# Forgetting attention of a streaming encoder: scores as two products with stacked query parts and the decay sums in rows of their own

## The chip, the cores and the metric

The kernel runs on one core of a Trainium2 chip. The metric is the device time of one execution in microseconds. A core has five engines with instruction queues of their own: PE (TensorE, matrix products; its weight loads are shown as PEld), DVE (VectorE), ACT (ScalarE), POOL (GpSimd) and SP (SyncE, which here only issues DMAs). Each engine works its queue in order. They wait for each other through semaphores.

## The reference

One step of a two-layer encoder: 512 new frames of a prompt stream and 32 frames of a running stream with 512 cached frames (544 frames in all, width 1024). The first layer has latent attention, the second forgetting attention, each between feed-forward blocks. What matters here is the second attention: 16 heads of width 64, and a logit bias that is the difference of two running sums of log forget gates.

```python
c_k = jnp.cumsum(logf_all, axis=1).transpose(0, 2, 1)
c_q = c_k[:, :, -l:]
q = _rms_norm((hn @ p['w_b_q'][j]).reshape(b, l, B_HEADS, B_HD), p['g_b_qn'][j])
o = _attention(q, k_all, v_all, pos, k_pos, False, c_q, c_k)
# in _attend:
s = jnp.einsum('bqhd,bkhd->bhqk', q, k, preferred_element_type=jnp.float32) * (q.shape[-1] ** -0.5)
s = s + (c_q[:, :, :, None] - c_k[:, :, None, :])
s = jnp.where(mask[None, None], s, -jnp.inf)
p = jax.nn.softmax(s, axis=-1).astype(v.dtype)
return jnp.einsum('bhqk,bkhd->bqhd', p, v)
```

The mask is causal by frame. The running stream's 32 frames attend to the 512 cached ones and to each other.

## The kernel before, in words

All arithmetic is in float32 accuracy on an engine path that rounds its operands. So every operand x is held as a high part (x rounded, made by ACT) and a low part (x minus the high part, made by DVE), and a product takes three matmuls: high by high, high by low, low by high. This is `product`, L600 to L604.

The kernel works in stages, each written as one program per engine: feed-forward F0, latent projection, first attention, output projection, F1, shared keys and values (KV), F2, query projection (Q), second attention, output projection, F3, final norm. Nothing reorders the instructions: what stands in a queue is the order in which the functions are called, and semaphore counts with names (`Steps`) tie the queues together.

The second attention is a loop over 8 pairs of heads (`pair_b` on PE, ACT, DVE and POOL; L1003, L1549, L2216, L2595, and the SP loop at L577). A turn p finishes pair p's second head (head 1), makes pair p + 1 ready ("staging") and does the scores of its first head (head 0):

- SP loads pair p + 1's keys and values from DRAM into SBUF, token by token (L571 to L574), each time after the buffer before it is free.
- PE turns keys and queries to have the head's width on the partitions (`staged`, L874; `staged_samples`, L882 for the 32 frames of the running stream); ACT and DVE split the result into high and low parts, `qT` and `kT` (`stage_part`, L1468 and L2126). In the profile `kT` is named x_hi and x_lo, whose memory it shares.
- Scores come in five groups u (`scores`, L885): u = 0 to 3 are four blocks of 128 queries against 128 x (u + 1) keys, u = 4 is the 32 running frames in two halves of 272 keys. Each group is a `product` and the mask, added by a matmul with the identity (L905, L912). DVE takes the row maximum (L2022), ACT the exponential (L1401), POOL divides by the row sum (L2571), PE turns the probabilities (L926), ACT and DVE split them, and PE multiplies them by the values (`values`, L946).
- The bias is inside the product: queries and keys have 66 rows, 64 of the head and two more. A query carries (1, sum at the query), a key (minus the sum at the key, 1). POOL copies the sums `cs` and `ncs` beside the heads (L2537, L2540), they are turned with them, and the gain column of the queries has ones in rows 64 and 65 (DVE memset at L1912).

Score groups use banks 0 to 2 of PSUM, and a group waits for the exponential of the group that had its bank before. The turns of keys, queries and probabilities share banks 3 to 5 (`w_uses`), and each waits for the splits of what the bank held.

The query projection ahead of it has eight units m of weights (L1147): PE multiplies five token tiles by the unit's weights, ACT rounds the next unit's weights (L1170), DVE makes their low part (L1722) and takes the finished half of the queries (L2336).

Of the kernel before, what the change touches and what calls it, by code (L numbers as in the profile page):

```python
# [19 lines left out]
ALU = mybir.AluOpType  # L20
# [20 lines left out]
DBX = DB + 2  # L41
# [37 lines left out]
class Steps:  # L79
# [81 lines left out]
    "dve": ["wlo", "fs0", "fs1", "b", "min", "u", "w", "z", "a", "wz", "rb", "eb", "l", "lf", "c", "negc"]}  # L161
FSTAGE = {"pool": ["q", "cq", "ck"]}
# [4 lines left out]
def build(nc, d):  # L167
    with ExitStack() as ctx:
# [81 lines left out]
        qn = place("q_normed", [P, NT, HEADS, DB])  # L250
        at_[0] = start + 4 * 7840
        cs = place("forget_sum", [P, NK, HEADS])
        ncs = place("forget_sum_neg", [P, NK, HEADS])
# [68 lines left out]
        def tile(t, k):  # L322
# [8 lines left out]
        k_loaded, v_loaded, stored = sem("k_loaded"), sem("v_loaded"), sem("stored")  # L331
        stored_lf = sem("stored_log_forget")
        stored_kv = [sem("stored_kv0"), sem("stored_kv1")]
        set_dve, set_act, set_pool = sem("setup_dve"), sem("setup_act"), sem("setup_pool")
# [4 lines left out]
                     forget=FORGET, fstage=FSTAGE, resplit=RESPLIT, relow=RELOW, yout=YOUT)  # L339
# [26 lines left out]
        def ffn(f, gain):  # L366
            parts = []
            for hf in range(HALVES):
# [4 lines left out]
                if hf == 1:  # L373
# [28 lines left out]
                 att=run("attx", PAIRS), out=run("out", PAIRS), fstage=run("fstage", PAIRS))  # L402
# [57 lines left out]
        def _(sp):  # L460
# [101 lines left out]
            ksx = ks[:, 0:NK * 2 * DBX].rearrange("p (t g w) -> p t g w", t=NK, g=2)  # L562
# [33 lines left out]
        def _(pe):  # L596
# [177 lines left out]
            pe.wait_ge(set_dve, 5)  # L774
# [39 lines left out]
            def attention(L, mla, mask):  # L814
                att, stg, stq, D = L["att"], L["stage"], L["stageq"], L["d"]
                prq, prk = L.get("projq"), L.get("projk")
                qsv = qs[:, 0:NT * 2 * D].rearrange("p (t g w) -> p t g w", t=NT, g=2)
                ksv = ks[:, 0:NK * 2 * D].rearrange("p (t g w) -> p t g w", t=NK, g=2)
# [42 lines left out]
                def staged(name, it, uses, before, first=False):  # L861

                    v, t0 = {"q": (qsv, 0), "p": (ksv, 0), "c": (ksv, NT)}[name[0]]
                    if not mla and name == "q0":
                        pe.wait_ge(*L["fstage"]["pool"].at("ck", it))
                        pe.wait_ge(k_loaded, 16 * 6 * (it + 1))
# [6 lines left out]
                    for t in range(4):  # L873
                        mm = pe.transpose(ps[0:D, b, t * P:(t + 1) * P], v[:, t0 + t, int(name[1]), :], ident[:, :])  # L874
                    mm.then_inc((stq if name[0] == "q" else stg)["pe"].sem, 1)

                def staged_samples(it, uses, before=None):
                    b = [x[1] for x in uses if x[0] == "ts"][0] if before is None else bank_of("ts", uses, before)
                    for n, v in enumerate((qsv, ksv)):
                        for g in range(2):  # L880
                            o = (2 * n + g) * DEC
                            mm = pe.transpose(ps[0:D, b, o:o + DEC], v[S0:P, 4, g, :], ident[S0:P, S0:P])  # L882
                    mm.then_inc(stg["pe"].sem, 1)

                def scores(hh, u, p, first=False):  # L885
# [14 lines left out]
                    q = [a[0:D, hh * T + TS[u]:hh * T + TS[u] + P] for a in qT]  # L900
                    k = [a[0:D, hh * KEYS:(hh + 1) * KEYS] for a in kT]
                    if u < 4:
                        out = ps[:, u % 3, 0:P_W[u]]
                        product(out, q, [a[:, 0:P_W[u]] for a in k], True, False)
                        mm = pe.matmul(out[:, u * P:(u + 1) * P], identr[:, :], mask[:, :], start=False, stop=True)  # L905
                    else:
                        for n in range(2):
                            c = SEQ + n * HALF_T
                            mm = product(ps[:, 1 + n, 0:HALF_T], q, [a[:, c:c + HALF_T] for a in k], True,
                                         mla or n == 0)  # L910
# [235 lines left out]

            for m in range(8):  # L1147
# [15 lines left out]
        def _(act):  # L1163
# [169 lines left out]
            act.wait_ge(set_dve, 7)  # L1333
# [53 lines left out]
            def attention(L, mla, g_q, g_k):  # L1387
# [74 lines left out]
                def stage_part(name, it, first=False):  # L1462
# [5 lines left out]
                    act.activation(out[0][0:D, hh * n + o:hh * n + o + SEQ], ps[0:D, b, :], ACT.Copy, **kw  # L1468
                                   ).then_inc(st["act"].sem, 1)

                def stage_samples(it, first=False):
                    inc, b = stg["act"].sem, (FIRST_BANKS if first else banks)["ts"]
                    act.wait_ge(*stg["pe"].at("ts", it))
                    for n, (out, g) in enumerate(((qT, g_q), (kT, g_k))):
                        w = T if n == 0 else KEYS
                        kw = {} if g is None else {"scale": g[0:D, :]}
                        act.activation(out[0][0:D, :].rearrange("p (g w) -> p g w", g=2)[:, :, w - DEC:w],
                                       ps[0:D, b, n * 2 * DEC:(n + 1) * 2 * DEC
                                          ].rearrange("p (g w) -> p g w", g=2), ACT.Copy, **kw).then_inc(inc, 1)

# [68 lines left out]
                def pair_b(p, first, stages):  # L1549
# [68 lines left out]
                else:  # L1618
                    for name in ("q0", "p0", "p1", "c0", "q1", "c1"):
                        stage_part(name, 0)  # L1620
                    stage_samples(0)
                    for u in range(5):
# [78 lines left out]
            for m in range(8):  # L1701
# [3 lines left out]
                if m == 5:  # L1705
                    square_queries(0)
            square_queries(1)
# [7 lines left out]
        def _(dve):  # L1715
# [196 lines left out]
            dve.memset(gbq[DB:DB + 2, :], 1.0).then_inc(set_dve, 1)  # L1912
# [97 lines left out]
            def attention(L, mla, g_q, g_k, meanwhile=None):  # L2010
# [109 lines left out]
                def stage_part(name, it, first=False):  # L2120
# [3 lines left out]
                    dve.wait_ge(*st["act"].at(name, it))  # L2124
                    c = slice(hh * n + o, hh * n + o + SEQ)
                    low(out[1][0:D, c], ps[0:D, b, :], out[0][0:D, c], None if g is None else g[0:D, :], st["dve"].sem)  # L2126

                def stage_samples(it, first=False):
                    b = (FIRST_BANKS if first else banks)["ts"]
                    for n, (out, g, w) in enumerate(((qT, g_q, T), (kT, g_k, KEYS))):  # L2130

                        dve.wait_ge(*stg["act"].at("sk", it))
                        o = [x[0:D, :].rearrange("p (g w) -> p g w", g=2)[:, :, w - DEC:w] for x in out]
                        low(o[1], ps[0:D, b, n * 2 * DEC:(n + 1) * 2 * DEC
                                     ].rearrange("p (g w) -> p g w", g=2), o[0],
                            None if g is None else g[0:D, :], stg["dve"].sem)
# [247 lines left out]
            for m in range(16):  # L2384
# [56 lines left out]
                if m == 10:  # L2441
# [4 lines left out]
                    dve.tensor_scalar(ncs[:, :, :], o, -1.0, None, ALU.mult).then_inc(finc, 1)  # L2446
# [21 lines left out]
            for m in range(8):  # L2468
# [11 lines left out]
                if m == 6:  # L2480
                    normalise(Q["k"][0], qv[0])
            take_chunk(Q["k"][1], U + 7, 1, qv[1].rearrange("p t g w -> p t (g w)"))
# [12 lines left out]
        def _(pool):  # L2495
# [30 lines left out]
            def attention(L, mla, meanwhile=None):  # L2526
                att, stg, D = L["att"], L["stage"], L["d"]
                prq, prk = L.get("projq"), L.get("projk")
                qsv = qs[:, 0:NT * 2 * D].rearrange("p (t g w) -> p t g w", t=NT, g=2)
                ksv = ks[:, 0:NK * 2 * D].rearrange("p (t g w) -> p t g w", t=NK, g=2)  # L2530

                def stage_fox(it):
# [6 lines left out]
                    for dst, src, n in ((qsv[:, :, :, DB + 1], cs, NT), (ksv[:, :, :, DB], ncs, NK)):  # L2539
                        pool.tensor_copy(dst, src[:, 0:n, bass.ds(it * 2, 2)]).then_inc(inc, 1)  # L2540
# [124 lines left out]
            qx = qs[:, 0:NT * 2 * DBX].rearrange("p (t w) -> p t w", w=DBX)  # L2665
            kx = ks[:, 0:NK * 2 * DBX].rearrange("p (t w) -> p t w", w=DBX)
            pool.memset(qx[:, :, DB:DB + 1], 1.0).then_inc(set_pool, 1)
            pool.memset(kx[:, :, DB + 1:DB + 2], 1.0).then_inc(set_pool, 1)
# [111 lines left out]
```

## Time and profile before

| | us |
|---|---|
| median of 3 runs | 2368.77 (2368.72 to 2372.03) |
| profiled execution, its own time | 2368.68 |
| span of the profile, first to last instruction | 2366.5 |
| busy: PE / DVE / ACT / POOL | 2233.0 / 1719.0 / 1076.0 / 322.4 |
| mean granted clock of PE | 0.972 of full speed |

The profile is of one execution. A timeline row gives the start of an instruction and how long it took; matmuls overlap in the array, so the time that one costs is the distance from its start to the next one's, not its duration. An idle time in brackets is that of the engine just before the instruction, with what ended it. "Granted clock" is the share of full speed at which PE was clocked; it has two levels here, 1.0 and 0.5 (2.4 and 1.2 GHz), and its column lags behind the matmuls by some us.

### The profile page before, as it was taken

How to read it: one execution, taken by the hardware profiler on the slowest of the kernel's cores; microseconds unless marked ns; L12 is line 12 of the kernel's file. 1: busy time of each engine (PE TensorE's matmuls, PEld its weight loads, DVE VectorE, ACT ScalarE, POOL GpSimd, SP SyncE). 2: the span in 40 equal slices, each digit the busy share in tenths (PEclk: the TensorE clock that was granted, in tenths of full speed). 3: DMA queues.
4: the chain of work that ended last, by engine and by line, in shares of the span. 5: the costliest groups of instructions: out<-in, count | busy, mean ns of one | idle time of the engine just before them, and what ended most of it. 6: DMA issues, size and time to landing. Idle time of an engine off the chain costs nothing. (4 is left out here: it accounts for less than half of the span.)

```text
span 2366.5 us, 45430 instructions
## 1 busy us (share of the span) xinstructions
PE 2233.0 (94%) x16514; PEld 2147.5 (91%) x16514; DVE 1719.0 (73%) x2708; ACT 1076.0 (45%) x1801; POOL 322.4 (14%) x281
## 2 busy tenths in 40 slices
PE   4999999889988899999999999999989998999997
PEld 4999999889988899999977999999868888999997
DVE  7985984578875896697455984995358858966973
ACT  5542543456764553354224551453247745533531
POOL 1000002035551100000122000001043321000001
PEclk9999999989988999999999999999979989999998
DMA  2222232100002232222223322222222212222221
GB/s 99 101 96 91 103 104 84 47 20 20 14 19 72 72 106 86 87 104 98 76 75 108 108 108 97 89 95 83 72 54 53 58 45 86 91 102 85 106 91 62
DMA packets 72801, 187.44 MB, mean 79 GB/s; under 512 B 40720, under 2 KB 42288, under 8 KB 61440
## 3 DMA queue, kind: packets, MB, share of 16 engines
q1 hardware_dynamic: 71424, 181.67, 22.7%
q0 software_dynamic: 1280, 4.49, 0.5%
q8 instruction: 59, 0.97, 0.2%
q14 instruction: 38, 0.31, 0.0%
HBM read 178.79 MB, written 7.35 MB: 79 GB/s over the span
## 5 line engine op out<-in xcount | busy, mean ns | idle before, releaser
L602 PE MATMUL ps<-xs_hi,w_hi 128*128 128x272 f32 x1408 | 410.3, 291 | 50.2 <-DVE w_lo_more L1752 31.9
L604 PE MATMUL ps<-xs_hi,w_lo 128*128 128x272 f32 x1408 | 408.0, 290 | 0.0
L603 PE MATMUL ps<-xs_lo,w_hi 128*128 128x272 f32 x1408 | 407.2, 289 | 0.0
L1170 ACT ACTIVATE w_hi<-raw 128x1408 fp32r<-128x1408 f32 (+4 forms) x123 | 146.0, 1188 | 506.1 <-PE ps L627 246.2
L1199 ACT ACTIVATE w_hi<-w_blocks 128x1024 fp32r<-128x1024 f32 x176 | 186.8, 1062 | 323.5 <-PE ps L604 157.8
L602 PEld LDWEIGHTS ps<-xs_hi,w_hi 128*128 128x128 f32 x1408 | 266.5, 189 | 54.1 <-issue 29.9
L602 PE MATMUL ps<-xs_hi,w_hi_more 128*128 128x272 f32 x1056 | 306.5, 290 | 2.4 <-ACT scratch L1245 1.8
L603 PE MATMUL ps<-xs_lo,w_hi_more 128*128 128x272 f32 x1056 | 305.9, 290 | 0.0
L627 PE MATMUL ps<-hid_hi,w_hi 128*128 128x272 f32 x1312 | 273.0, 289 | 9.1 <-DVE w_lo L1722 5.4
L627 PE MATMUL ps<-hid_lo,w_hi 128*128 128x272 f32 x1312 | 271.9, 289 | 0.0
L627 PE MATMUL ps<-hid_hi,w_lo 128*128 128x272 f32 x1312 | 271.8, 289 | 0.0
L604 PEld LDWEIGHTS ps<-xs_hi,w_lo 128*128 128x128 f32 x1408 | 267.1, 190 | 0.0
L603 PEld LDWEIGHTS ps<-xs_lo,w_hi 128*128 128x128 f32 x1408 | 266.7, 189 | 0.0
L1752 DVE TENSOR_TENSOR w_lo<-w_blocks,w_hi 128x1024 fp32r<-128x1024 f32 x176 | 215.2, 1223 | 28.3 <-ACT w_hi L1199 26.7
L1874 DVE SCALAR_TENSOR_TENSOR scratch<-ps,rstd 128x544 f32<-128x544 f32 x64 | 46.3, 724 | 257.0 <-PE ps L627 223.9
L627 PEld LDWEIGHTS ps<-hid_hi,w_hi 128*128 128x128 f32 x1312 | 207.4, 189 | 11.1 <-issue 11.1
L1722 DVE TENSOR_TENSOR w_lo<-raw,w_hi 128x1408 fp32r<-128x1408 f32 (+4 forms) x123 | 170.3, 1386 | 58.0 <-ACT w_hi L1170 57.8
L627 PEld LDWEIGHTS ps<-hid_hi,w_lo 128*128 128x128 f32 x1312 | 207.4, 189 | 0.0
L627 PEld LDWEIGHTS ps<-hid_lo,w_hi 128*128 128x128 f32 x1312 | 207.3, 189 | 0.0
L602 PEld LDWEIGHTS ps<-xs_hi,w_hi_more 128*128 128x128 f32 x1056 | 200.6, 190 | 3.9 <-ACT scratch L1245 2.7
L604 PE MATMUL ps<-xs_hi,w_lo_more 128*128 128x272 f32 x704 | 204.0, 290 | 0.0
L603 PEld LDWEIGHTS ps<-xs_lo,w_hi_more 128*128 128x128 f32 x1056 | 200.3, 190 | 0.1
(261 smaller groups left out, 5069.1 us busy)
## 6 DMA issues: line engine op xcount, KB each, us to landing
w_blocks<-w_ffn_in SPq DMA_DIRECT2D x88, 1024.0 KB, 4.8
raw<-w_ffn_out SPq DMA_DIRECT2D x64, 704.0 KB, 4.1
raw<-w_b_kv SPq DMA_DIRECT2D x16, 512.0 KB, 3.6
raw<-w_a_out SPq DMA_DIRECT2D x8, 512.0 KB, 3.6
raw<-w_b_q SPq DMA_DIRECT2D x8, 512.0 KB, 3.5
raw<-w_b_out SPq DMA_DIRECT2D x8, 512.0 KB, 3.6
raw<-w_a_in SPq DMA_DIRECT2D x4, 672.0 KB, 4.0
raw<-w_a_qup SPq DMA_DIRECT2D x8, 288.0 KB, 2.8
```

Source lines behind the costliest of these rows:

```text
L602: pe.matmul(out, lhs[0], rhs[0], start=start, stop=False, skip_group_check=more)
L603: pe.matmul(out, lhs[0], rhs[1], start=False, stop=False, skip_group_check=more)
L604: return pe.matmul(out, lhs[1], rhs[0], start=False, stop=stop, skip_group_check=more)
L627: mm = pe.matmul(pair(bank)[:, n, :], w[a], xs[b][:, cols], start=(k == 0 and a + b == 0), stop=(k == kt - 1 and a == 1))
L1170: act.activation(wh[par][:, 0:n], raw[par][:, 0:n], ACT.Copy).then_inc(w_hi, 1)
L1199: act.activation(wgroup[name][0], sources(par, name), ACT.Copy).then_inc(q["ws"]["act"].sem, 1)
L1722: dve.tensor_tensor(wl[par][:, 0:n], raw[par][:, 0:n], wh[par][:, 0:n].bitcast(F32), ALU.subtract).then_inc(w_lo, 1)
L1752: dve.tensor_tensor(lo, sources(par, name), hi.bitcast(F32), ALU.subtract).then_inc(q["ws"]["dve"].sem, 1)
L1874: dve.scalar_tensor_tensor(two(scratch[2]), pair(2 + j), -0.5, two(rstd[:, :]), ALU.mult, ALU.mult).then_inc(inc, 1)
```

## The change

Only the second attention and what prepares it is touched.

- Queries: rows 0 to 63 of `qT[0]` hold the high part and rows 64 to 127 the low part. `qT[1]` holds the high part again in rows 0 to 63 and two rows of decay sums and two of -1 behind them. ACT rounds the queries into `qT[1]`, DVE writes the low part into the lower half of `qT[0]`, and ACT copies the high part over (`queries_twice`, two copies of 64 x 544 a pair).
- Keys: SP loads each key twice, side by side, so that the turned keys have 128 rows; `kT[0]` has the high part in both halves. `kT[1]` has the low part in rows 0 to 63, two rows of ones and two of decay sums.
- Scores: `qT[0]` by `kT[0]` (128 rows) and `qT[1]` by `kT[1]` (68 rows): two matmuls for what took three. The product's decay terms are (sum at the query, high and low) x 1 and -1 x (sum at the key, high and low).
- Decay sums: in the query projection PE turns `cs` (`turn_decay`, three steps after units 3, 4 and 5), ACT and DVE split it, SP stores both parts in DRAM, and in each turn of its loop SP loads the pair's rows into `kT[1]` and `qT[1]` with six DMAs, after PE's last score group of the pair before. PE waits for them ahead of the first score of head 0.
- POOL no longer copies sums beside the heads; `ncs` is gone. It fills the rows of ones.

```diff
-DBX = DB + 2
+DBX = 2 * DB
+DBK = DB + 4
...
+        q_heads = place("q_heads", [P, NT, 2, DB + 2])[:, :, :, :]
+        k_heads = arena[:, 0:NK * 4 * DB].rearrange("p (t g w) -> p t g w", t=NK, g=2)
+        at_[0] = start + 4 * 6400
+        decay = [at_col("decay_hi", C_ARENA + nq + nk + nv, KEYS, F32R)[0:HEADS, :],
+                 place("decay_lo", [HEADS, KEYS], F32R)[:, :]]
         at_[0] = start + 4 * 7840
         cs = place("forget_sum", [P, NK, HEADS])
-        ncs = place("forget_sum_neg", [P, NK, HEADS])
...
-                    sp.dma_start(dst[:, 0:4, g, 0:DB], d[new_p].rearrange("(t p) e -> p t e", p=P)[:, :, cols]
-                                 ).then_inc(loaded_, 16)
-                    sp.dma_start(dst[S0:P, 4, g, 0:DB], d[new_s][:, cols]).then_inc(loaded_, 16)
-                    sp.dma_start(dst[:, NT:NK, g, 0:DB], d[old].rearrange("(t p) e -> p t e", p=P)[:, :, cols]
-                                 ).then_inc(loaded_, 16)
+                    for to, src in ((dst[:, 0:4, g], d[new_p].rearrange("(t p) e -> p t e", p=P)[:, :, cols]),
+                                    (dst[S0:P, 4, g], d[new_s][:, cols]),
+                                    (dst[:, NT:NK, g], d[old].rearrange("(t p) e -> p t e", p=P)[:, :, cols])):
+                        for n in range(to.shape[-1] // DB):
+                            sp.dma_start(to[..., n * DB:(n + 1) * DB], src).then_inc(loaded_, 16)
+
+            sp.wait_ge(*X["decay"]["dve"].at("sample"))
+            for n in range(2):
+                sp.dma_start(d["decay"][n], decay[n][:, :].bitcast(F32)).then_inc(decay_stored, 16)
...
+                sp.wait_ge(decay_stored, 32)
+                sp.wait_ge(decay_ones, 3)
+                sp.wait_ge(*X["att"]["pe"].at("s14", p - 1))
+                for n in range(2):
+                    heads = d["decay"][n:n + 1, bass.ds(2 * p, 2), :]
+                    rows = kT[1][DB + 2 + n:DB + 3 + n, :].bitcast(F32).rearrange("p (g w) -> p g w", g=2)
+                    sp.dma_start(rows, heads).then_inc(decay_loaded, 16)
+                    rows = qT[1][DB + n:DB + n + 1, :].bitcast(F32).rearrange("p (g w) -> p g w", g=2)
+                    for o, c, w in ((0, 0, SEQ), (SEQ, SEQ + PAST, DEC)):
+                        sp.dma_start(rows[:, :, o:o + w], heads[:, :, c:c + w]).then_inc(decay_loaded, 16)
...
-                    q = [a[0:D, hh * T + TS[u]:hh * T + TS[u] + P] for a in qT]
-                    k = [a[0:D, hh * KEYS:(hh + 1) * KEYS] for a in kT]
+                    if not mla and hh == 0 and u == 0:
+
+                        pe.wait_ge(decay_loaded, 16 * 6 * (p + 1))
+                    if not mla and u == 0:
+                        pe.wait_ge(*L["twice"]["act"].at(f"q{hh}", p))
+                    rows = (D, D) if mla else (P, DBK)
+                    q = [a[0:r, hh * T + TS[u]:hh * T + TS[u] + P] for a, r in zip(qT, rows)]
+                    k = [a[0:r, hh * KEYS:(hh + 1) * KEYS] for a, r in zip(kT, rows)]
+
+                    def times(out, k, stop):
+                        if mla:
+                            return product(out, q, k, True, stop)
+                        pe.matmul(out, q[0], k[0], start=True, stop=False)
+                        return pe.matmul(out, q[1], k[1], start=False, stop=stop)
+
                     if u < 4:
                         out = ps[:, u % 3, 0:P_W[u]]
-                        product(out, q, [a[:, 0:P_W[u]] for a in k], True, False)
+                        times(out, [a[:, 0:P_W[u]] for a in k], False)
...
+            def turn_decay(n):
+
+                st = X["decay"]
+                if n == 0:
+                    pe.wait_ge(*Q["rtok"]["dve"].at("rtok"))
+                else:
+                    pe.wait_ge(*st["dve"].at(DECAY["dve"][n - 1]))
+                if n < 2:
+                    for t in range(4):
+                        mm = pe.transpose(ps[0:HEADS, MISC, t * P:(t + 1) * P], cs[:, t if n == 0 else NT + t, :],
+                                          ident[:, :])
+                else:
+                    mm = pe.transpose(ps[0:HEADS, MISC, 0:DEC], cs[S0:P, 4, :], ident[S0:P, S0:P])
+                mm.then_inc(st["pe"].sem, 1)
...
+                if m in (3, 4, 5):
+                    turn_decay(m - 3)
...
+                def queries_twice(hh, it):
+
+                    act.wait_ge(*stq["act"].at(f"q{hh}", it))
+                    act.wait_ge(*stg["act"].at("sq", it))
+                    c = slice(hh * T, (hh + 1) * T)
+                    act.activation(qT[0][0:DB, c], qT[1][0:DB, c], ACT.Copy).then_inc(L["twice"]["act"].sem, 1)
...
                         stage_samples(p + 1)
+                        queries_twice(0, p + 1)
                     split_p(1, 0, p)
+                    if stages:
+                        queries_twice(1, p + 1)
...
+                    n, name = m - 3, DECAY["act"][m - 3]
+                    act.wait_ge(*X["decay"]["pe"].at(name))
+                    o, w = (n * SEQ, SEQ) if n < 2 else (SEQ + PAST, DEC)
+                    act.activation(decay[0][:, o:o + w], ps[0:HEADS, MISC, 0:w], ACT.Copy
+                                   ).then_inc(X["decay"]["act"].sem, 1)
...
+                    elif name[0] == "q":
+                        dve.wait_ge(*st["act"].at(name, it))
+                        low(out[0][DB:P, c], ps[0:DB, b, :], out[1][0:DB, c], g[0:DB, :], st["dve"].sem)
+                    else:
+                        dve.wait_ge(*st["act"].at(name, it))
+                        low(out[1][0:DB, c], ps[0:DB, b, :], out[0][0:DB, c], None, st["dve"].sem)
...
+                    n, name = m - 3, DECAY["dve"][m - 3]
+                    dve.wait_ge(*X["decay"]["act"].at(name))
+                    o, w = (n * SEQ, SEQ) if n < 2 else (SEQ + PAST, DEC)
+                    low(decay[1][:, o:o + w], ps[0:HEADS, MISC, 0:w], decay[0][:, o:o + w], None, X["decay"]["dve"].sem)
...
-                    for dst, src, n in ((qsv[:, :, :, DB + 1], cs, NT), (ksv[:, :, :, DB], ncs, NK)):
-                        pool.tensor_copy(dst, src[:, 0:n, bass.ds(it * 2, 2)]).then_inc(inc, 1)
...
+                    pool.wait_ge(*L["fstage"]["pool"].at("q", 0))
+                    pool.memset(kT[1][DB:DBK, :].bitcast(F32), 1.0).then_inc(decay_ones, 1)
+                    pool.wait_ge(decay_ones, 3)
```

The order of the instructions was read in three places. First SP, its loop over the pairs, before:

```order
L571 DMA arena<-o_k_p 128x4x64
L573 DMA arena<-o_k_s 32x64
L574 DMA arena<-fox_k 128x4x64
L582 REGISTER_ALU
L571 DMA arena<-o_v_p 128x4x64 [waits stagev_pool]
L573 DMA arena<-o_v_s 32x64
L574 DMA arena<-fox_v 128x4x64
L571 DMA arena<-o_v_p 128x4x64
L573 DMA arena<-o_v_s 32x64
L574 DMA arena<-fox_v 128x4x64
L577 REGISTER_ALU
L577 COMPARE_AND_BRANCH
```

and after; `decay` is the DRAM copy of the sums, `x_lo` is `kT[1]`:

```order
L585 DMA arena<-fox_v 128x4x64
L601 ISA [waits decay_ones,decay_stored]
L605 ISA [waits attx_pe]
L605 DMA x_lo<-decay 1x2112
L608 DMA qT_lo<-decay 1x2x512
L608 ISA
L608 DMA qT_lo<-decay 1x2x32
L605 ISA
L605 DMA x_lo<-decay 1x2112
L608 DMA qT_lo<-decay 1x2x512
L608 ISA
L608 DMA qT_lo<-decay 1x2x32
```

Six loads of decay rows now stand behind the six loads of values (only the last of these is shown here) in each turn, with waits for `decay_ones`, `decay_stored` and PE's last score group of the pair before; the key loads, ahead of the values, are twelve.

Second PE, the first score group of the next pair in a turn, before:

```order
L926 MATMUL ps<-ident,arena 128x128 [waits stage_dve]
L926 MATMUL ps<-ident,arena 128x128 x2
L899 REGISTER_ALU [waits attx_act]
L602 MATMUL ps<-x_hi,qT_hi 128x128 [waits stage_dve]
L603 MATMUL ps<-x_lo,qT_hi 128x128
L604 MATMUL ps<-x_hi,qT_lo 128x128
L905 MATMUL ps<-mask_causal,identr 128x128
L926 MATMUL ps<-ident,arena 128x128 [waits stage_dve]
```

and after:

```order
L968 MATMUL ps<-ident,arena 128x128 [waits stage_dve]
L968 MATMUL ps<-ident,arena 128x128 x2
L929 REGISTER_ALU [waits attx_act]
L932 REGISTER_ALU [waits stage_dve]
L934 REGISTER_ALU [waits decay_loaded]
L942 MATMUL ps<-x_hi,qT_hi 128x128 [waits twice_act]
L943 MATMUL ps<-x_lo,qT_lo 128x128
L948 MATMUL ps<-mask_causal,identr 128x128
L968 MATMUL ps<-ident,arena 128x128 [waits stage_dve]
```

The third matmul of a group is gone, and a wait for `decay_loaded` stands ahead of the first. The rest of PE's queue is behind it, the next score groups and the value products of head 1 among them.

Third ACT, in the query projection, with rounding of weights (`w_hi`) and squares of the queries, before:

```order
L1170 ACTIVATE w_hi<-raw_49 128x1024 [waits w_used,w_load0]
L1170 ACTIVATE w_hi<-raw_50 128x1024 [waits w_used,w_load1]
L1170 ACTIVATE w_hi<-raw_49 128x1024 [waits w_used,w_load0]
L1170 ACTIVATE w_hi<-raw_50 128x1024 [waits w_used,w_load1]
L1170 ACTIVATE w_hi<-raw_49 128x1024 [waits w_used,w_load0]
L1647 ACTIVATE scratch<-q_normed 128x2048 [waits tokq_dve]
L1649 ACTIVATE rstd<-q_normed 128x512
L1170 ACTIVATE w_hi<-raw_50 128x1024 [waits w_used,w_load1]
```

and after:

```order
L1229 ACTIVATE w_hi<-raw_50 128x1024 [waits w_used,w_load1]
L1229 ACTIVATE w_hi<-raw_49 128x1024 [waits w_used,w_load0]
L1788 ACTIVATE decay_hi<-ps 16x512 [waits decay_pe]
L1229 ACTIVATE w_hi<-raw_50 128x1024 [waits w_used,w_load1]
L1788 ACTIVATE decay_hi<-ps 16x512 [waits decay_pe]
L1229 ACTIVATE w_hi<-raw_49 128x1024 [waits w_used,w_load0]
L1724 ACTIVATE scratch<-q_normed 128x2048 [waits tokq_dve]
L1726 ACTIVATE rstd<-q_normed 128x512
```

ACT's first copy of decay sums stands ahead of the rounding of a unit's weights, the second ahead of the next.

## Rows read from the trace of the kernel before

**Rows 1.** Stages: one of six alike of the second attention's loop
```profile
core 0: us, PE busy (x) PEld busy (x) DVE busy (x) ACT busy (x) POOL busy (x), PEclk, DMA share, GB/s
...
1880.00:1900.00 20.00, 18.91 (x141) 16.54 (x141) 16.25 (x43) 15.01 (x42) 6.83 (x9) 1.00 0.22 54
```
**Rows 2.** Timeline of PE: start us, us, engine line op out<-in [idle before <-releaser]
```profile
1780.09 0.33 PE L602 MATMUL ps<-x_hi,qT_hi 66*128 66x128 f32 x1
...
1800.01 0.33 PE L602 MATMUL ps<-x_hi,qT_hi 66*128 66x128 f32 x1
...
1809.82 0.44 PE L602 MATMUL ps<-hid_hi,x_hi 128*128 128x384 f32 x1 [0.57 <-DVE x_lo L1732]
...
1812.24 0.30 PE L602 MATMUL ps<-x_hi,qT_hi 66*128 66x128 f32 x1
...
1812.49 0.28 PE L604 MATMUL ps<-x_hi,qT_lo 66*128 66x128 f32 x1
1812.60 0.28 PE L905 MATMUL ps<-mask_causal,identr 128*128 128x128 f32 x1
...
1815.23 0.39 PE L604 MATMUL ps<-x_hi,qT_lo 66*128 66x512 f32 x1
1815.46 0.23 PE L905 MATMUL ps<-mask_causal,identr 128*128 128x128 f32 x1
...
1816.89 0.28 PE L604 MATMUL ps<-x_hi,qT_lo 66*128 66x272 f32 x1
1817.01 0.18 PE L912 MATMUL ps<-mask_causal,identr 128*128 128x32 f32 x1
...
1899.50 0.33 PE L602 MATMUL ps<-x_hi,qT_hi 66*128 66x128 f32 x1
```
**Rows 3.** Timeline of DVE in the same turn
```profile
1802.74 0.56 DVE L2022 TENSOR_REDUCE stat<-ps 128x1 f32<-128x384 f32 x1 [0.26 <-PE ps L905]
...
1816.96 0.28 DVE L1732 TENSOR_TENSOR hid_lo<-ps,hid_hi 128x128 fp32r<-128x128 f32 x1
```
**Rows 4.** Timelines of ACT and of POOL in the same turn
```profile
1804.53 0.62 ACT L1460 ACTIVATE x_hi<-arena 128x512 fp32r<-128x512 f32 x1
...
1812.27 0.98 ACT L1410 ACTIVATE hid_hi<-ps 128x512 fp32r<-128x512 f32 x2 [0.95 <-PE ps L926]
...
1805.23 1.28 POOL L2577 TENSOR_TENSOR x_lo<-arena,x_hi 128x512 fp32r<-128x512 f32 x1 [5.74 <-ACT x_hi L1460]
```
**Rows 5.** Timeline of SP in the same turn, first and last of six value loads
```profile
1806.54 0.37 SPq L571 DMA_DIRECT2D arena<-o_v_p  x1
...
1809.12 0.38 SPq L574 DMA_DIRECT2D arena<-fox_v  x1
```
**Rows 6.** DMA issues from 1780 to 1900 us: count, KB each, median us to landing
```profile
arena<-fox_v SPq DMA_DIRECT2D x12, 128.0 KB, 2.5
...
arena<-o_v_s SPq DMA_DIRECT2D x12, 8.0 KB, 2.0
```
**Rows 7.** Timelines of PE and of ACT ahead of and in turn 0
```profile
1704.64 0.50 PE L602 MATMUL ps<-w_hi,x_hi 128*128 128x512 f32 x1 [0.35 <-DVE q_normed L2336]
...
1765.90 0.77 PE L602 MATMUL ps<-hid_hi,x_hi 128*128 128x512 f32 x1 [4.66 <-POOL x_lo L2577]
...
1701.60 1.06 ACT L1170 ACTIVATE w_hi<-raw 128x1024 fp32r<-128x1024 f32 x1 [7.01 <-PE ps L604]
```
**Rows 8.** Two holes of PE, and stages: mean granted clock is PEclk
```profile
1233.87 0.50 PE L602 MATMUL ps<-w_hi,x_hi 128*128 128x512 f32 x1 [3.10 <-DVE kv_chunk L2336]
...
1299.99 0.36 PE L602 MATMUL ps<-xs_hi,w_hi 128*128 128x272 f32 x1 [3.32 <-DVE w_lo_more L1752]
...
1234.00:1254.00 20.00, 20.00 (x102) 17.45 (x103) 10.22 (x9) 4.35 (x3) 6.79 (x1) 0.88 0.27 83
1300.00:1320.00 20.00, 19.59 (x140) 19.18 (x141) 18.60 (x25) 10.31 (x16) 1.31 (x2) 0.91 0.35 113
1744.00:1772.00 28.00, 22.08 (x94) 18.40 (x93) 15.84 (x35) 12.17 (x31) 19.81 (x16) 0.57 0.10 23
```

More of the change, by code:

```diff
@@ L338, in build @@
                      stage=STAGE, stageq=STAGEQ, projq=PROJQ, projk=PROJK, first=FIRST, latent=LATENT, tokn=TOKN, tokq=TOKQ, tokq1=TOKQ1, tokv=TOKV, rtok=RTOK,
-                     forget=FORGET, fstage=FSTAGE, resplit=RESPLIT, relow=RELOW, yout=YOUT)
+                     forget=FORGET, fstage=FSTAGE, twice=TWICE, decay=DECAY, resplit=RESPLIT, relow=RELOW, yout=YOUT)
         sems = {(k, e): sem(f"{k}_{e}") for k, v in kinds.items() for e in v}
@@ L401, in build @@
         X = dict(d=DBX, stage=run("stage", PAIRS), stageq=run("stageq", PAIRS), stagev=run("stagev", PAIRS), head0=run("head0x", PAIRS),
-                 att=run("attx", PAIRS), out=run("out", PAIRS), fstage=run("fstage", PAIRS))
+                 att=run("attx", PAIRS), out=run("out", PAIRS), fstage=run("fstage", PAIRS),
+                 decay=run("decay"), twice=run("twice", PAIRS))
         XO = dict(kind="out", what="supdate", u=units(KC, KC * P), kt=KC, st=run("supdate", DK),
@@ L771, in token_rstd @@
                 mm.then_inc(step.sem, 1)
-            pe.wait_ge(set_dve, 5)
+            pe.wait_ge(set_dve, 4)
             ffn_all(F0)
@@ L908, in scores @@
                             c = SEQ + n * HALF_T
-                            mm = product(ps[:, 1 + n, 0:HALF_T], q, [a[:, c:c + HALF_T] for a in k], True,
-                                         mla or n == 0)
+                            mm = times(ps[:, 1 + n, 0:HALF_T], [a[:, c:c + HALF_T] for a in k], mla or n == 0)
                         if not mla:
@@ L1467, in stage_part @@
                     kw = {} if g is None else {"scale": g[0:D, :]}
-                    act.activation(out[0][0:D, hh * n + o:hh * n + o + SEQ], ps[0:D, b, :], ACT.Copy, **kw
-                                   ).then_inc(st["act"].sem, 1)
+                    c = slice(hh * n + o, hh * n + o + SEQ)
+                    if mla or name[0] != "q":
+                        act.activation(out[0][0:D, c], ps[0:D, b, :], ACT.Copy, **kw).then_inc(st["act"].sem, 1)
+                    else:
+                        act.activation(out[1][0:DB, c], ps[0:DB, b, :], ACT.Copy, scale=g[0:DB, :]
+                                       ).then_inc(st["act"].sem, 1)
                 def stage_samples(it, first=False):
@@ L1621, in attention @@
                     stage_samples(0)
+                    queries_twice(0, 0)
+                    queries_twice(1, 0)
                     for u in range(5):
@@ L2132, in stage_samples @@
                         dve.wait_ge(*stg["act"].at("sk", it))
[L2133 to L2136, printed above, removed]
+                        o = [x.rearrange("p (g w) -> p g w", g=2)[:, :, w - DEC:w] for x in out]
+                        if mla:
+                            r, o = slice(0, D), [x[0:D] for x in o]
+                        else:
+                            r, o = slice(0, DB), [o[1][0:DB], o[0][DB:P]] if n == 0 else [x[0:DB] for x in o]
+                        low(o[1], ps[r, b, n * 2 * DEC:(n + 1) * 2 * DEC].rearrange("p (g w) -> p g w", g=2), o[0],
+                            None if g is None else g[r, :], stg["dve"].sem)
                 def split_units(it):
@@ L2664, in _ @@
             pool.wait_ge(*KV["k"][1]["dve"].at("ss"))
[L2665 to L2668, printed above, removed]
+            pool.wait_ge(*Q["rms"]["pe"].at("stat"))
+            pool.memset(qT[1][DB:DBK, :].bitcast(F32), -1.0).then_inc(decay_ones, 1)
+            pool.wait_ge(decay_ones, 1)
+            pool.memset(q_heads[:, :, :, DB:DB + 2], 0.0).then_inc(decay_ones, 1)
             pool.memset(vrv[0:S0, 4], 0.0).then_inc(vpad, 1)
@@ L2771 @@
     d |= {n: nc.dram_tensor(n, s, F32, kind="ExternalOutput").ap() for n, s in OUTS.items()}
+    d["decay"] = nc.dram_tensor("decay", (2, HEADS, KEYS), F32, kind="Internal").ap()
     build(nc, d)
```

56 lines of the change are left out of this document (36 added, 20 removed).

## The prediction

> **What bounds the kernel now.** I read the stages first: from 1780 to 1900 us six stretches of 20 us are all but alike, with PE busy 18.9 us of 20 at a granted clock of 1.00, DVE 16.2, ACT 15.0 [rows 1] (the last of the six). Then the timeline of PE inside one stretch. The loop of the second attention handles a pair of heads per turn. I call T0 the start of the first score of head 1 in a turn. T0 is 1780.09 in one turn, 1800.01 in the next and 1899.50 six turns after the first [rows 2], so a turn takes (1899.50 - 1780.09) / 6 = 19.90 us. PE has few holes: the last matmul before the value product of 384 columns waited 0.57 us for DVE's x_lo [rows 2]. So the turn is bounded by PE with DVE close behind.
>
> **The removed product.** In each score group the third product (L604) goes. Its price is the distance to the next start, since matmuls overlap: 0.11 us for 128 columns (1812.49 to 1812.60), 0.23 for 512 (1815.23 to 1815.46), 0.12 for 272 (1816.89 to 1817.01) [rows 2]. Widths 256 and 384 lie between: I take 0.11 and 0.18. A head has 128, 256, 384, 512 and twice 272: 0.11 + 0.11 + 0.18 + 0.23 + 0.24 = 0.87 us, 1.74 a turn. Eight turns would give 14 us if PE alone set the time. The two products that stay have 128 and 68 rows in place of 66. The distances above go by columns, so I price the taller operands at 0, between -0.1 and +0.1 a turn.
>
> **How much of that reaches the end of a turn.** I cut the turn at the first score of the next pair (head 0, group 0), which starts at 1812.24, that is T0 + 12.23 [rows 2]. Ahead of it 0.87 us of products go. But DVE sets this part: after its last short wait (0.26 us for PE at 1802.74, [rows 3]) it runs without a hole of note until the staged keys are split, and PE's wait at 1809.82 is for that. DVE can start at most that 0.26 earlier, plus about 0.1 for group 0: PE comes to T0 + 11.9. Behind the cut there are 19.90 - 12.23 = 7.67 us. 0.87 us of products go here too, but the last value products wait for DVE's low half of the turned probabilities, which ends at 1816.96 + 0.28 = 1817.24 [rows 3], just ahead of them. Its chain (four row maxima, three splits) begins with the first score and gets shorter only by what PE delays in it. Bounds: 6.8 (all 0.87) and 7.67 (nothing); I take 7.1, about two thirds of the saving.
>
> **The added loads on SP.** This is the term that decides. A turn of SP was: six loads of keys, a wait for POOL's split of the values, six loads of values. Now twelve, wait, six, and then six rows of decay sums, whose landing the first score of the next pair waits for. SP issues in order, so these six stand behind the six value loads. When do the value loads start? ACT copies the values at 1804.53 for 0.62 us, POOL splits them from 1805.23 for 1.28 us, and SP issues its first value load at 1806.54, T0 + 6.53 [rows 4, 5]. Nothing of the change makes that earlier: ACT works without a hole from the turn's start to there. The last value load is issued at 1809.12 + 0.38 = 1809.50; six loads thus take 2.96 us, 0.53 from one to the next [rows 5]. The decay rows: six DMAs, the last one issued 5 x 0.53 = 2.65 us after the first, the first 0.1 us after the values. Landing: an 8 KB load lands 2.0 us after its issue, a 128 KB load 2.5 us [rows 6]; a decay row (at most 8.4 KB) is nearest to the first. Another 0.2 us until PE starts. From the first value load: 2.96 + 0.1 + 2.65 + 2.0 + 0.2 = 7.9 us, so the first score starts at T0 + 6.53 + 7.9 = T0 + 14.4, while PE is there at T0 + 11.9. PE waits 2.5 us, and DVE and ACT, whose next row maximum and exponential hang on this score, with it. A turn becomes 14.4 + 7.1 = 21.5 us, 1.6 more than 19.9. No trace shows the issue of a DMA into one partition: bounds are 0.45 us each with 1.8 to land (T0 + 13.9) and 0.6 each with 3.0 to land (T0 + 15.8).
>
> **The other edits of a turn.** ACT gets two copies of queries, 64 x 544 from SBUF; the copy of 512 columns took 0.62 us [rows 4], so 0.65 each. The first falls into ACT's hole of 0.95 us at 1812.27 [rows 4], the second behind it, both while PE waits for the decay rows: 0 us; without that cover the first would still end at about T0 + 11.95, where PE comes, and cost at most 0.3. The doubled keys turn with the same transposes (moving operand is the identity, 128 columns) and the same ACT copy, 512 columns: 0. POOL loses two short copies that nobody waits for: 0. Twelve key loads on SP start behind the decay rows, at about T0 + 12.5, take 6.4 us and have landed by T0 + 21.5; staging asks for them in the following turn, behind four score groups: 0.
>
> **Ahead of the loop.** The decay sums are turned during the query projection: nine transposes on PE, at 0.1 us each 0.9 us. The first four sit after unit 3, and ACT's first decay copy (16 x 512, priced like a 512-column copy, 0.6 us) stands ahead of the split of unit 5's weights, which starts at 1701.60 and leads through DVE's split to the take of the projected queries; DVE has a low half of its own ahead of that. PE already waits there 0.35 us at 1704.64 [rows 7]. PE's transposes 0.5, ACT 0.6 and about 0.1 of handover push that chain by 1.2 us, and it is on the path. The other five transposes add 0.6: +1.8 us. POOL's memset of the ones rows (about 2.2 us) and the first decay loads end near 1740, before the first score of pair 0: 0. Then come five score groups at half clock (mean granted clock 0.57 from 1744 to 1772, [rows 8]), where a product costs double: (0.11 + 0.11 + 0.18) x 2 = 0.8 us up to group 2, on whose exponential group 4 waits for its bank, and 0.48 in group 4, together -1.3, of which ACT's two copies ahead of the first exponential take back 0.1: -1.2. So PE's long wait for POOL, ending at 1765.90 [rows 7], moves by +0.6. From there the value loads of pair 1 begin (0.2 us earlier than PE starts), 1766.3, plus 7.9 gives the first score at 1774.2, plus 7.1 gives T0 of turn 1 at 1781.3 against 1780.09: +1.2. Six turns: 6 x 1.6 = 9.9 us (unrounded 1.65). The last turn stages nothing and waits for values and DVE: 0. Sum +11.1 us. The profiled execution took 2368.68 us (span 2366.5 and 2.2 around it), the median of the runs is 2368.77: 2379.8, rounded 2380.
>
> **Rivals.**
> B, the clock: a hole of 2.5 us of PE in every turn lets the granted clock fall. For: after a hole of 3.32 us at 1299.99 the mean clock over the next 20 us was 0.91. Against: after 3.10 us at 1233.87 it was 0.88 in the next 20 us though the fall there came late, and holes of 0.6 us leave it at 1.00 [rows 8, 1]. So holes near 3 us stand at the edge. The clock's fall shows in the stretch behind the hole, which is the 7.1 us that PE mostly sets; 0.91 over 20 us is 3.6 us at half clock, and as much or twice that behind each hole would add 1.8 to 2.5 us a turn (not all of a turn's end is PE's), in six turns +13: 2393. The Trainium skill (TensorE: Matmul & The Clock Gate, HAM oscillation) says that a loop whose every tile waits for a DMA starts every tile at the lower of the two clocks; by that rule B would be the case in each turn, and the traces so far bear it out in part.
> C, the other side: the decay rows land before PE asks. It decides at T0 + 11.9, that is 5.4 us after the first value load; the value loads take 2.96 and the landing 2.0, which leaves 0.4 us for six issues, against 0.53 for one. If it held (or if SP ran its wait for the values much earlier than now), a turn would gain 0.3 + 0.6 = 0.9 us: +0.6 - 0.6 - 6 x 0.9 = -5.4, 2363.
> D, the PE saving is small and the wait hidden in part (issue and landing at their lower bounds, tail 6.8): a turn 20.7, +0.8: with the prologue about 2374.
>
> **Numbers.** A with its bounds 55 in 100 (own range 2374 to 2391), B 22, D 13, C 10. The range holds A, B and most of D: 2370 to 2397. A measurement of this kernel tells 0.2%, 4.7 us, from no change. C is mostly faster (0.08), the lower end of D and upper end of C same (0.08), the rest slower (0.84).
>
> **What would show it.** Right: in the timeline of PE a hole of 2 to 3.5 us ahead of the first score of head 0 in each turn, named as waiting for a DMA into x_lo or qT_lo; SP's value loads at T0 + 6.5 with six decay loads behind them; turns of 21 to 22.5 us; the score groups with two products at the distances above. The clock column decides between A and B: 1.00 or below 0.9 in the turns. Wrong: turns below 19.9 us, or decay loads that land before T0 + 12; a wait ahead of the first score that names ACT's copy of queries would show another cause; a shift of more than 3 us at the first transposes of pair 0 would show the decay turns mispriced.

## The result, and the profile after

| | us |
|---|---|
| before, median of the runs beside it | 2368.74 (2368.30 to 2372.03) |
| after, median of 4 runs | 2394.18 (2391.41 to 2405.25) |
| ratio after to before | 1.0116, 95% interval 1.0099 to 1.0133 |
| profiled execution of after, span, mean clock of PE | 2393.64, 2391.7, 0.964 |

The change makes the kernel 25.4 us slower. The forecast was slower by 11, to 2380. The direction and the place are as forecast, and the size is more than double. I read the profile after in the order of before: stages, then PE in one turn, then the queue that PE waits for. Three stretches of 23 us, each about a turn long, have the columns of [rows 1]:

```profile
core 0: us, PE busy (x) PEld busy (x) DVE busy (x) ACT busy (x) POOL busy (x), PEclk, DMA share, GB/s
1783.00:1806.00 23.00, 18.95 (x128) 16.25 (x126) 16.75 (x43) 15.80 (x43) 7.56 (x10) 0.93 0.32 72
...
1829.00:1852.00 23.00, 19.42 (x121) 16.61 (x120) 16.83 (x43) 15.81 (x43) 7.59 (x10) 0.85 0.32 72
...
1875.00:1898.00 23.00, 19.41 (x123) 16.43 (x122) 16.26 (x42) 15.10 (x43) 6.83 (x10) 0.87 0.30 67
```

A turn takes 23.1 to 25.7 us where it took 19.9, every engine has more idle time, and the granted clock, 1.00 before, is 0.93 in the first two of the six turns and falls to 0.78 in the last. The timeline of PE shows both causes a few rows apart. T0 of this turn is 1805.82:

```profile
1805.82 0.33 PE L942 MATMUL ps<-x_hi,qT_hi 128*128 128x128 f32 x1
...
1808.45 0.50 PE L942 MATMUL ps<-x_hi,qT_hi 128*128 128x512 f32 x1 [0.34 <-ACT arena L1460]
1808.78 0.39 PE L943 MATMUL ps<-x_lo,qT_lo 68*128 68x512 f32 x1
1809.01 0.22 PE L948 MATMUL ps<-mask_causal,identr 128*128 128x128 f32 x1
...
1815.25 0.44 PE L627 MATMUL ps<-hid_hi,x_hi 128*128 128x384 f32 x1 [0.54 <-DVE x_lo L1815]
...
1820.35 0.32 PE L942 MATMUL ps<-x_hi,qT_hi 128*128 128x128 f32 x1 [2.37 <-DMA qT_lo<-decay]
...
1821.33 0.63 PE L942 MATMUL ps<-x_hi,qT_hi 128*128 128x384 f32 x1
1821.75 0.52 PE L943 MATMUL ps<-x_lo,qT_lo 68*128 68x384 f32 x1
1822.07 0.31 PE L948 MATMUL ps<-mask_causal,identr 128*128 128x128 f32 x1
```

First, PE waits 2.37 us for a decay row ahead of head 0's first score (1820.35, T0 + 14.53). Over the six turns these waits sum to 14.0 us:

```profile
engine line waited for: us in total, times, longest us
...
PE ps L942 <- DMA qT_lo<-decay: 14.0, 6, 2.4
```

Second, behind the hole matmuls take longer. A product of 384 columns starts 0.42 us ahead of its successor (1821.33 to 1821.75) and a 68-row one 0.32; in the same turn ahead of the hole they take 0.25 and 0.18 (1807.45, 1807.70, 1807.88). That is the lower of the two clock levels; from about 1824.5 the distances are the short ones again. Asked for single microseconds, the clock column says the same: 1.00 up to 1821, then 0.59, 0.50, 0.50 and 0.70, and 1.00 from 1825. So in this trace it does not lag behind the matmuls, as I had written of it ahead of the prediction; over a stretch of 20 us it only blurs where the fall was. The queue that PE waits for, SP, in the same turn, answers to [rows 5]:

```profile
1812.21 0.37 SPq L585 DMA_DIRECT2D arena<-o_v_p  x1
...
1814.80 0.38 SPq L585 DMA_DIRECT2D arena<-fox_v  x1
1815.50 0.25 SPq L605 DMA_DIRECT2D x_lo<-decay  x1
1815.84 1.39 SPq L608 DMA_DIRECT2D qT_lo<-decay  x2
1817.42 0.27 SPq L605 DMA_DIRECT2D x_lo<-decay  x1
1817.78 1.33 SPq L608 DMA_DIRECT2D qT_lo<-decay  x2
```

The value loads start at T0 + 6.39, and the six decay rows stand behind them.

### The profile page after: what moved, and what is told of

It reads as the page before. It is cut to its first block and busy times, and to the rows that moved or that the text cites. A ratio compares the mean times of both kernels' runs of the same rounds, so it can differ in the third digit from the quotient of the medians.

```text
span 2391.7 us, 45537 instructions
## 1 busy us (share of the span) xinstructions
PE 2239.7 (94%) x16427; PEld 2151.3 (90%) x16427; DVE 1724.2 (72%) x2709; ACT 1085.2 (45%) x1820; POOL 323.3 (14%) x266
```

## The experiments

T0 and the first score of head 0, X, are read in each as in the prediction: X - T0 is the head of a turn, from X to the next T0 its tail. Before: 12.2 and 7.7. After, in the six turns: heads 14.5 in five and 16.1, tails 8.6, 8.6, 9.6, 9.5, 10.7, 9.6. These are the rows, T0 and X by turns (the three between 1797.20 and 1843.45 are 1805.82 and 1820.35, above, and T0 = 1828.93):

```profile
1782.68 0.33 PE L942 MATMUL ps<-x_hi,qT_hi 128*128 128x128 f32 x1
1797.20 0.40 PE L942 MATMUL ps<-x_hi,qT_hi 128*128 128x128 f32 x1 [2.28 <-DMA qT_lo<-decay]
...
1843.45 0.32 PE L942 MATMUL ps<-x_hi,qT_hi 128*128 128x128 f32 x1 [2.36 <-DMA qT_lo<-decay]
1853.00 0.33 PE L942 MATMUL ps<-x_hi,qT_hi 128*128 128x128 f32 x1
1867.52 0.32 PE L942 MATMUL ps<-x_hi,qT_hi 128*128 128x128 f32 x1 [2.37 <-DMA qT_lo<-decay]
1877.06 0.33 PE L942 MATMUL ps<-x_hi,qT_hi 128*128 128x128 f32 x1
1891.57 0.32 PE L942 MATMUL ps<-x_hi,qT_hi 128*128 128x128 f32 x1 [2.36 <-DMA qT_lo<-decay]
1902.27 0.47 PE L942 MATMUL ps<-x_hi,qT_hi 128*128 128x128 f32 x1
1918.40 0.32 PE L942 MATMUL ps<-x_hi,qT_hi 128*128 128x128 f32 x1 [2.26 <-DMA qT_lo<-decay]
1927.96 0.33 PE L942 MATMUL ps<-x_hi,qT_hi 128*128 128x128 f32 x1
```

The head of 16.1 us follows the tail of 10.7: there the clock was at the lower level from 1892.9 to 1906.5, past T0.

There are two theories of the tail: K, the clock falls behind the hole; its rivals, other work that the change adds. And two of the head: Q, the rows' place in SP's queue; its rivals, ACT's copies or DVE. The runs of before beside the kernels with half of the filler, with both edits and with the later copy had the median 2368.19 us, those beside the other four 2368.91.

**The decay rows ahead of the values** (5 rounds). The six loads and their waits move, in SP's loop:

```diff
                 load_heads(p, k_loaded, "o_k_p", "o_k_s", "fox_k", ksx)
+                (the waits and the six loads of decay rows)
                 sp.wait_ge(*X["stagev"]["pool"].at("v", p - 1))
                 load_heads(p, v_loaded, "o_v_p", "o_v_s", "fox_v", vsx)
-                (the waits and the six loads of decay rows)
```

> The changed kernel with SP's six loads of decay rows issued ahead of its six loads of values in each turn; nothing else. Theory Q (place in SP's queue): the decay rows are issued from about T0 + 5.6, have landed by T0 + 11.5, PE's hole of 2.4 us ahead of the first score of head 0 is gone, the clock stays at 1.00, a turn takes 12.0 + 7.1 = 19.1 us against 23.1 to 25.2 now, and the time is 2363 to 2367 us, below the kernel before. Rival F (the new form itself costs: taller operands, two ACT copies, doubled keys): turns stay above 21 us and the time above 2380.

Measured: 2366.08 us, ratio 0.9989 (0.9980 to 0.9998). SP and PE in one turn, with T0 at 1798.49:

```profile
1804.23 0.25 SPq L602 DMA_DIRECT2D x_lo<-decay  x1
...
1808.07 0.41 SPq L585 DMA_DIRECT2D arena<-o_v_p  x1
```
```profile
1798.49 0.33 PE L942 MATMUL ps<-x_hi,qT_hi 128*128 128x128 f32 x1
...
1810.40 0.31 PE L942 MATMUL ps<-x_hi,qT_hi 128*128 128x128 f32 x1
...
1817.79 0.33 PE L942 MATMUL ps<-x_hi,qT_hi 128*128 128x128 f32 x1
```

The decay rows go out at T0 + 5.7, no wait is left ahead of X, the head is 11.9, the tail 7.4, a turn 19.3, and the clock stays at 1.00 in the six turns. Q is shown: the same loads at another place in the queue cost nothing. The values, now 3.2 us later from T0 (9.58 against 6.39), hold nobody up.

**A filler in the hole** (3 rounds). Eleven matmuls, whose results nothing reads, keep PE busy until the decay rows land:

```diff
                     if stages:
+                        for _ in range(11):
+                            pe.matmul(ps[:, 7, 64:512], identr[:, :], wh[0][:, 0:448], start=True, stop=True)
                         scores(0, 0, p + 1)
```

> The changed kernel with eleven extra matmuls of 448 columns (identity by a weight tile, into unused columns of bank 7, results never read), about 2.25 us, where PE waits for the decay rows. Theory K (half of the loss is the clock that falls after the hole): the first score still starts at T0 + 14.5, but the rest of the turn takes 7.1 us in place of 8.6 to 10.7, a turn is 21.6 us, and the time is 2379 to 2383. Rival (the rest of the turn is slow for another reason than the clock): 2392 to 2396, as the changed kernel.

Measured: 2379.98 us, ratio 1.0043 (1.0027 to 1.0059). One turn:

```profile
1806.35 0.33 PE L942 MATMUL ps<-x_hi,qT_hi 128*128 128x128 f32 x1
...
1820.91 0.32 PE L942 MATMUL ps<-x_hi,qT_hi 128*128 128x128 f32 x1
...
1827.95 0.33 PE L942 MATMUL ps<-x_hi,qT_hi 128*128 128x128 f32 x1
```

The head stays (14.56), since the rows land no sooner. But each tail is 7.03 to 7.06 us, the granted clock is 1.00 in all six turns, and PE, given more work, ends 14 us earlier. K is shown: of the 25 us, about 14 are the clock. The other 11 are the wait, less what the removed products save.

**Half of the filler** (3 rounds), `range(5)` in place of `range(11)`:

> The changed kernel with five matmuls of 448 columns (about 1 us), whose result nothing reads, ahead of the first score of head 0. PE's hole ahead of that score shrinks from 2.4 us to about 1.4. If the clock falls only behind holes as long as 2.4 us, the tails stay at 7.1 and the total is 2380, as with eleven such matmuls. If every hole above about 1 us brings the half clock, the tails stay at 8.6 to 10.7 and the total is 2392 to 2396. In between, 2383 to 2390, if only some turns fall.

Measured: 2376.59 us, ratio 1.0036 (1.0024 to 1.0048).

```profile
1814.83 0.32 PE L942 MATMUL ps<-x_hi,qT_hi 128*128 128x128 f32 x1 [1.36 <-DMA qT_lo<-decay]
...
1821.87 0.33 PE L942 MATMUL ps<-x_hi,qT_hi 128*128 128x128 f32 x1
```

Holes of 1.25 to 1.36 us in every turn leave the tails at 7.04 to 7.06 and the clock at 1.00; holes of 2.3 to 2.4 us in the same place bring the lower clock in every turn. The time is 3.4 us below that with the whole filler, but the six turns together take the same in both profiles (129.4 and 129.8 us), so this difference is not theirs.

The Trainium skill (TensorE: Matmul & The Clock Gate, HAM oscillation) describes a loop with DMA waits of about 3 to 5 us in which every tile starts at the lower clock. The holes here are shorter than those waits: the one of 2.37 us brings the lower clock all the same, though only 0.8 us behind X, and the one of 1.36 us does not. No run here has a wait of 3 to 5 us in each turn.

The size of the hole is not all that decides. In the kernels with three loads and with both edits, below, the clock falls once in the first of the six turns (0.50 from 1787.0 to 1790.4, and from 1785.8 to 1789.2). In both the waits ahead of that fall are 0.34 and 0.51 us; the kernel with the rows first has 0.33 and 0.51 at the same scores of that turn and keeps 1.00. What else decides is open.

**The loads alone** (3 rounds). The kernel before, with its three products, gets six loads of the same sizes into spare rows that nothing reads, behind the value loads, and PE waits for them ahead of the same score (PE's part of the edit; SP's six loads are left out here):

```diff
+                    if not mla and hh == 0 and u == 0:
+                        pe.wait_ge(extra_loaded, 16 * 6 * (p + 1))
                     q = [a[0:D, hh * T + TS[u]:hh * T + TS[u] + P] for a in qT]
```

> The kernel before, with its scores of three products, plus six small loads into unused rows behind the values in SP's queue and PE's wait for them ahead of the first score of head 0. Theory Q: these loads and the wait alone cost what the change cost, and more by the third products: first score at T0 + 14.5, a tail of 7.7 us at full clock or 9 to 11 with the clock's fall, a turn of 23.5 to 25.5 us, the time 2392 to 2402. Rival F: the time stays near 2369 to 2375, since the wait would hide in what DVE and ACT take.

Measured: 2405.87 us, ratio 1.0156 (1.0140 to 1.0171).

```profile
1798.72 0.45 PE L613 MATMUL ps<-x_hi,qT_hi 66*128 66x128 f32 x1 [2.09 <-DMA spare_q<-x]
1812.08 0.47 PE L613 MATMUL ps<-x_hi,qT_hi 66*128 66x128 f32 x1
1829.13 0.33 PE L613 MATMUL ps<-x_hi,qT_hi 66*128 66x128 f32 x1
1836.82 0.33 PE L613 MATMUL ps<-x_hi,qT_hi 66*128 66x128 f32 x1
```

Loads and wait alone cost 37 us, more than the whole change and more than I expected (2392 to 2402); the rest of the change takes 12 us off again. Turns of 24.5 to 28 us alternate: the first tail here, 13.4 us, is all at the lower clock (a product's own time is 0.45 to 0.47), the second, 7.7 us, at the higher one, but its head took 17.05. The granted clock is at the lower level from 1798.2 to 1825.5, so a slow stretch can reach far into the head of the next turn. That also suggests why the turns alternate: behind such a slow head PE comes to X when the loads have landed (no wait stands at 1829.13), the clock stays up behind it, and the next turn is fast enough to have the hole again (2.08 us). No run tests this.

**Three loads in place of six** (5 rounds), at the place of the change. Both parts of the sums come with one DMA into two partitions (the first rows of the edit; the query rows change alike, and PE waits for three loads):

```diff
-                for n in range(2):
-                    heads = d["decay"][n:n + 1, bass.ds(2 * p, 2), :]
-                    rows = kT[1][DB + 2 + n:DB + 3 + n, :] ...
+                heads = d["decay"][:, bass.ds(2 * p, 2), :]
+                rows = kT[1][DB + 2:DB + 4, :] ...
```

> The changed kernel with the decay rows of a turn loaded by three DMAs (two partitions each) in place of six, at the same place behind the values. Theory Q with 0.55 to 0.65 us per issue: the first score moves from T0 + 14.5 to about T0 + 12.8, the hole is 0.7 us and the clock stays up: a turn of 19.9 us, time 2368 to 2373. Rival (landing and not issue sets the hole): first score still after T0 + 14, time above 2385.

Measured: 2365.84 us, ratio 0.9988 (0.9979 to 0.9997). SP's three issues, and PE:

```profile
1811.72 0.26 SPq L604 DMA_DIRECT2D x_lo<-decay  x1
1812.08 0.70 SPq L607 DMA_DIRECT2D qT_lo<-decay  x2
```
```profile
1802.05 0.33 PE L941 MATMUL ps<-x_hi,qT_hi 128*128 128x128 f32 x1
1814.41 0.32 PE L941 MATMUL ps<-x_hi,qT_hi 128*128 128x128 f32 x1 [0.21 <-DMA qT_lo<-decay]
1821.44 0.33 PE L941 MATMUL ps<-x_hi,qT_hi 128*128 128x128 f32 x1
```

SP starts them at T0 + 9.67 as in the changed kernel (9.68), but is done after 1.06 us and not 3.6. In five of the six turns X moves up by 2.1 us, to T0 + 12.4, a wait of 0.2 to 0.3 us for the rows is left, and the tails are 7.03 to 7.07; the first turn has the fall of the clock told above, a head of 13.2 and a tail of 7.3. I had expected T0 + 12.8 and 2368 to 2373 us. The same bytes in half as many DMAs are worth 28 us.

**Both edits together, rows first and three loads** (5 rounds):

> The decay rows stand ahead of the value loads and come in three loads of two rows each (both edits at once). Theory Q (only the landing of the decay rows against PE's arrival matters): once the rows have landed before PE asks, fewer loads bring nothing more: first score of head 0 at T0 + 11.9 without a DMA wait, turn 19.3, total 2366, like the kernel with the decay rows ahead of the values. Rival (SP's queue is itself short of time, so that value and key loads come late): 2 us fewer issues per turn show as 0.2 to 0.5 us a turn, total 2363 to 2364.

Measured: 2364.66 us, ratio 0.9986 (0.9977 to 0.9995), heads 11.91 and turns of 19.29 but for the first turn, 13.16 and 20.41, with the fall of the clock told above. From the second turn on it is the kernel with the rows first; the 1.4 us between the totals are within the spread of the runs. The rival expected a turn shorter by 0.2 to 0.5 us, and none is: SP is not short of time.

**And ACT's second copy later** (5 rounds), on top of both:

```diff
                     split_p(1, 0, p)
-                    if stages:
-                        queries_twice(1, p + 1)
...
                         exp(0, 4, p + 1)
+                        queries_twice(1, p + 1)
```

> The kernel with the decay rows ahead of the values and in three loads, and ACT's second copy of queries (head 1) moved behind the last exponential of head 0, where ACT had a hole of 0.9 to 1.2 us. Theory F (in the kernel with the decay rows first, this copy of 0.6 us stands ahead of the first exponentials and makes the part behind the first score 7.38 us in place of 7.05): the part falls to 7.0 to 7.1, a turn to 19.0, total about 2364. Rival (DVE sets that part alone): it stays at 7.4, total 2366.

Measured: 2361.47 us, ratio 0.9967 (0.9955 to 0.9979), the fastest of all, 6.7 us faster than before.

```profile
1798.38 0.33 PE L941 MATMUL ps<-x_hi,qT_hi 128*128 128x128 f32 x1
1810.16 0.31 PE L941 MATMUL ps<-x_hi,qT_hi 128*128 128x128 f32 x1
1817.53 0.33 PE L941 MATMUL ps<-x_hi,qT_hi 128*128 128x128 f32 x1
```

Theory F fails in its place: the tail stays at 7.37. The turn is 0.12 shorter all the same (19.17), and that is in the head, 11.78 for 11.91. The trace points to DVE for the tail: ACT now waits 0.58, 0.17 and 0.88 us for DVE's row maxima in it. No run tests that. The total is 3.2 us below the kernel without this edit. In the profiles the six turns give 1.8 of it (116.88 and 115.08 us), of which 1.2 are the first turn, where the clock does not fall here. The rest I can't place; part may be the spread of the stages ahead of the loop, below.

## Why the prediction was wrong in size

By its own steps, with what the trace of after shows:

- **The removed product**: right. Where 0.11 and 0.23 us were priced for a third product, the two that stay keep their distances (68 rows by 512 columns 0.23, 1808.78 to 1809.01).
- **PE at X without the wait, T0 + 11.9**: right, 11.9 with the rows first. DVE has no wait there between 1799.46 and 1810.76, and PE's longest, 0.54 us, is for it. In the rows before I had passed over two more short waits of DVE, 0.23 and 0.33 us; they change nothing here.
- **The decay rows, X at T0 + 14.4**: right, 14.5 in five turns. Its terms were off against each other: the value loads began 0.1 us sooner and the first decay row went out 0.3 us behind them, not 0.1; the six issues took 3.6 us (1815.50 to 1819.11; 0.35 for a key row, 0.7 for each query load) where 2.65 up to the start of the last were priced, and PE started 1.2 us behind the end of the last, where 2.2 behind its start were priced. Heads: (88.73 - 73.4) = +15.3 us over six turns where 13.0 were forecast; 1.6 of the difference is the sixth head, 16.13, which began at the lower clock.
- **The tail at 7.1 us**: this is the step that failed. It holds at the full clock (7.03 to 7.06 with the hole filled; 7.05 behind turn 0, whose hole is 1.09 us). But the holes of 2.4 us brought the lower clock, and the tails sum to 56.6 us where 42.6 were forecast: 14 us, as much as the total was off by (the other differences cancel but for 0.4 us). The likeliest case had to be rival B. I weighed its two rows, holes of 3.10 and 3.32 us at the edge [rows 8], against holes of 0.6 us, and took 2.5 for the safe side. Those were single holes; here one comes in each turn. And only one of the two rows spoke of its hole: behind 1299.99 the clock is down from 1300.5 to 1304, but the 0.88 behind 1233.87 is a fall at 1249.3, 15 us later. B's own price, 1.8 to 2.5 us a turn and 2393 in total, fits: the tails are 1.5 to 3.6 us over 7.1.
- **Ahead of the loop**: T0 of turn 1 is 2.6 us later (1782.68). The first transposes of pair 0 are 3.3 us later (1733.47 and 1736.74), past the 3 us that I had named as a sign of mispriced decay turns, but 1.7 us of this stand already at 1671, ahead of those turns. And the six other kernels with this same stage start their first transposes anywhere from 1732.3 to 1738.0. One trace can't tell the forecast +1.2 from nothing, nor confirm +1.8 for the decay turns.
- **The last turn at 0**: wrong by 2.8 us. From its T0 to the output projection (1927.96 to 1946.55) it took 18.59 us in place of 21.36 before. It has no decay wait, and before, 12.8 us of it ran at the lower clock, after, 3.4.

The sum for after: +2.6 at T0 of turn 1, +25.9 in six turns, -2.8 in the last, -0.5 behind it: +25.2 in the span. Of the rivals, C holds as a mechanism: with the rows landed, a turn gained 0.6 us (forecast 0.9, since the tail is then 7.4 and not 7.1) and the total 2.8 (forecast 5.4). D's place, a wait nearly hidden, is the kernel with three loads, though its tails come at 7.05 and its turn at 19.5.

## What to carry to other kernels

An added load is priced by its place in an in-order queue, not by its bytes: ask who waits for it, what is ahead of it, and how many DMAs it is split into. A hole that returns in each turn of a loop bounded by PE can be paid twice, once as the wait and once as the lower clock behind it (here the holes of 2.3 us were, those of 1.4 us were not), so the time behind it must not be priced at full clock unless a trace shows a hole of that size, in that rhythm, leaving the clock up. When such a loss is found, moving or merging the loads is worth more than the work that they were meant to save: here the change without its wait gave 3 to 7 us, and the order and number of a few small loads decided between that and a loss of 25.

## What the hardware showed that I had not expected

- Holes of 1.25 to 1.36 us in turns of 21.6 us leave the clock at 2.4 GHz. Holes of 2.3 to 2.4 us in turns of 23.1 to 25.7 us bring 1.2 GHz, from 0.1 to 1.8 us behind the hole and for 3.4 to 13.7 us.
- The clock can stay down while PE works. In the kernel with the loads alone one fall lasted 27.3 us (1798.2 to 1825.5), and PE was busy for 24.8 of the 25 us from 1812 to 1837.
- More PE work made the kernel faster: eleven matmuls a turn, with no use for the result, gained 14 us; five matmuls a turn, 18 us.
- SP needed 1.39 us for two query loads of one part of the sums (one partition each), but 0.70 us for two that bring both parts into two partitions; a 128 KB value load took 0.37 to 0.46. Why a load into one partition takes the longer is open.
